# Decoder layer on one core: two stores moved ahead of loads in the SyncE queue, and the VectorE, ScalarE and TensorE lists reordered at the seams and in the last norm

## The reference

```
xn  = rms_norm(x, g_mix);  q, k, v, h, B, C = split(xn @ w_in)
mix = concat(dilated_attention(q, k, v), B * conv3(C * h)) @ w_out
h1  = x + mix
hn  = rms_norm(h1, g_ffn)
y   = h1 + (silu(hn @ w_gate) * (hn @ w_up)) @ w_down
out = rms_norm(y, g_final)
```

## Time and profile before

| | before |
|---|---|
| median of 3 executions | 1271.15 us (1271.0 to 1271.72) |
| the profiled execution, its own time | 1269.17 us |
| span of its instructions | 1267.4 us |
| PE busy | 1228.7 us, 97% of the span |
| DVE, POOL, ACT busy | 46%, 39%, 33% |
| mean granted clock of PE | 0.992 of full speed |
| chain that ended last, by engine | PE 84%, DVE 7%, issue 3%, DMA 2%, ACT 2%, POOL 1% |

### The profile page before, as it was taken

How to read it: one execution, slowest core, us unless ns; L and a number is a source line. 1 busy time by engine, 2 the same in 40 slices (tenths; PEclk the granted TensorE clock), 3 DMA queues, 4 the chain that set the end, 5 groups by cost and what they waited for, 6 DMA issues and landing times.

```text
span 1267.4 us, 22504 instructions
## 1 busy us (share of the span) xinstructions
PE 1228.7 (97%) x9232; PEld 1137.0 (90%) x9232; DVE 579.8 (46%) x982; ACT 418.7 (33%) x806; POOL 494.6 (39%) x414
## 2 busy tenths in 40 slices
PE   7999999999999999999699999999999999999997
PEld 7998778889755599999699999999999999999997
DVE  6844313424666523478233333322111178755665
ACT  6000110000577711255233333333333343444441
POOL 3454023233133132041578777776777650000000
PEclk9999999999999999999799999999999999999999
DMA  5545367353122041001334546454131495222223
GB/s 205 180 167 209 114 221 259 120 185 115 50 67 67 2 172 67 1 26 43 133 123 166 197 159 198 163 183 131 56 101 51 150 353 193 91 92 92 78 75 103
DMA packets 59989, 163.55 MB, mean 129 GB/s; under 512 B 6448, under 2 KB 19952, under 8 KB 55664
## 3 DMA queue, kind: packets, MB, share of 16 engines
q1 hardware_dynamic: 59888, 162.12, 36.9%
HBM read 127.81 MB, written 34.28 MB: 128 GB/s over the span
## 4 chain that ended last, share of the span: by engine, by line
PE 84%; DVE 7%; issue 3%; DMA 2%; ACT 2%; POOL 1%; SPq 1%; DVEq 0%; ACTq 0%; POOLq 0%
PE ps L1283 10%; PE ps L1285 10%; PE ps L1284 10%; PE ps L853 6%; PE ps L855 6%; PE ps L854 6%; PE ps L1309 5%; PE ps L1310 5%; PE ps L1311 5%; PE ps L993 3%; PE ps L1036 3%; PE ps L1060 2%; PE ps L1061 2%; PE ps L1062 2%; PE ps L1015 2%
## 5 line engine op out<-in xcount | busy, mean ns | idle before, releaser
L1283 PE MATMUL ps<-combo,w_hi 128*128 128x264 f32 x672 | 193.0, 287 | 16.2 <-ACT evac L1381 13.8
L1285 PE MATMUL ps<-combo,w_lo 128*128 128x264 f32 x672 | 192.2, 286 | 0.0
L1284 PE MATMUL ps<-combo,w_hi 128*128 128x264 f32 x672 | 192.0, 286 | 0.0
L853 PE MATMUL ps<-act_hi,w_hi 128*128 128x352 f32 x480 | 158.7, 331 | 7.9 <-DVE act_lo L1829 7.9
L855 PE MATMUL ps<-act_hi,w_lo 128*128 128x352 f32 x480 | 154.9, 323 | 0.0
L854 PE MATMUL ps<-act_lo,w_hi 128*128 128x352 f32 x480 | 154.8, 323 | 0.0
L1309 PE MATMUL ps<-hid,w_hi 128*128 128x264 f32 x536 | 152.9, 285 | 1.5 <-DVE resid L2230 1.5
L1310 PE MATMUL ps<-hid,w_hi 128*128 128x264 f32 x536 | 152.4, 284 | 0.0
L1311 PE MATMUL ps<-hid,w_lo 128*128 128x264 f32 x536 | 152.3, 284 | 0.0
L771 POOL TENSOR_TENSOR w_lo<-w_stage,w_hi 128x512 fp32r<-128x512 f32 (+1 forms) x71 | 97.6, 1375 | 138.4 <-ACT w_hi L1381 138.3
L1283 PEld LDWEIGHTS ps<-combo,w_hi 128*128 128x128 f32 x672 | 127.8, 190 | 16.9 <-issue 16.8
(11 more groups left out here) (393 smaller groups left out, 2953.1 us busy)
## 6 DMA issues: line engine op xcount, KB each, us to landing
w_stage<-in_w SPq DMA_DIRECT2D x61, 512.0 KB, 4.2
resid<-in_state_k SPq DMA_DIRECT2D x8, 1792.0 KB, 7.4
v_buf<-in_state_v SPq DMA_DIRECT2D x14, 1024.0 KB, 5.0
h_d<-evac SPq DMA_DIRECT2D x44, 264.0 KB, 3.1
norms<-in_w SPq DMA_DIRECT2D x22, 512.0 KB, 4.3
t_d<-norms SPq DMA_DIRECT2D x11, 1024.0 KB, 7.8
resid<-in_xT SPq DMA_DIRECT2D x16, 528.0 KB, 8.3
raw<-in_w SPq DMA_DIRECT2D x14, 512.0 KB, 4.4
```

The lines of the kernel that those rows point to most:

```text
L853: pe.matmul(out, hi, rhs_hi, start=first, stop=False)
L1283: pe.matmul(out, hi[:, wk], x_hi[:, k, tk], start=(k == 0 and first), stop=False, skip_group_check=not first)
L1284: pe.matmul(out, hi[:, wk], x_lo[:, k, tk], start=False, stop=False, skip_group_check=not first)
L1285: mm = pe.matmul(out, lo[:, wk], x_hi[:, k, tk], start=False, stop=(k == 3), skip_group_check=not first)
```

## The change

The order of work is changed in five places; no operation of the computation is added or removed. (1) At the start of the gate products the SP queue loads gate(2) before it waits for the first SwiGLU values, stores `(1, 0)` and `(1, 1)` ahead of loads that they stood behind, and puts the four `load_sums` transfers behind both stores and two more weight loads. (2) On DVE `plain_hidden` moves from behind six `combined` to behind the first. (3) At the seam to the down product ACT runs `keep_u2` of the last slice before `down_highs(0)` (the rest of the ACT diff there is the same list written out), SP issues `load_hidden("a11", 0)` before two `load_down`, and DVE runs `put_down(0, m)` one step earlier. (4) Under P2, P7 and P4 the squares of quarter 0 move to behind step 49, an ACT square root of one column is added behind step 48, `last_rows(0)` moves from k = 5 to k = 6 and `last_normals(0)` is done in one piece behind step 60. (5) Under the second pass of P4 `last_columns(2)` moves from the end of tile 0 to its step 8, `last_rows(2)` from the end of tile 1 to its step 6, and ACT and DVE take the squares of quarter 2 before the root and mean of quarter 1.

```diff
--- before.py
+++ after.py
@@ -592,16 +592,21 @@
                     source = t_d[k][:, 512 * W_SUMS[product]:512 * W_SUMS[product] + 512]
                 sp.dma_start(down_words(s), source).then_inc(down_in[n % DOWN_RAWS], 16)
 
-            for i in range(4):
+            for i in range(5):
                 load_gate(i)
-            for f in range(1, FT):
+            store_hidden(0, 0)
+            store_hidden(1, 0)
+            load_gate(5)
+            load_gate(6)
+            store_hidden(1, 1)
+            load_gate(7)
+            store_hidden(0, 1)
+            load_gate(8)
+            sp.wait_ge(dve_lo, 32)
+            load_sums(0)
+            load_sums(1)
+            for f in range(3, FT):
                 store_hidden(0, f - 1)
-                if f == 1:
-                    load_gate(4)
-                if f == 2:
-                    sp.wait_ge(dve_lo, 32)
-                    load_sums(0)
-                    load_sums(1)
                 if f < FT - 1:
                     load_gate(2 * f + 3)
                 store_hidden(1, f - 1)
@@ -619,13 +624,13 @@
             split_ready(sp, (FT - 2, "P7"))
             load_down(0)
             load_down(1)
+            sp.wait_ge(gate_done, GATE_NO[FT - 1, "P1"])
+            load_hidden("a11", 0)
             split_ready(sp, (FT - 1, "P5"))
             load_down(2)
             split_ready(sp, (FT - 1, "P6"))
             sp.wait_ge(t_made, 4 * (FT - 1))
             load_down(3)
-            sp.wait_ge(gate_done, GATE_NO[FT - 1, "P1"])
-            load_hidden("a11", 0)
             split_ready(sp, (FT - 1, "P4"))
             load_down(4)
             load_down(5)
@@ -1356,7 +1361,7 @@
                     mm.then_inc(step_done, 1)
                 if k == 3:
                     last_columns(0)
-                if k == 5:
+                if k == 6:
                     last_rows(0)
             down_product(5)
             first_pass(6)
@@ -1365,12 +1370,13 @@
                     mm = down_tile(6 * HK + k, m, 1)
                     if (m, k) == (0, 3):
                         last_columns(1)
+                    if (m, k) == (0, 8):
+                        last_columns(2)
+                    if (m, k) == (1, 6):
+                        last_rows(2)
                 mm.then_inc(tile_done, 1)
                 if m == 0:
                     last_rows(1)
-                    last_columns(2)
-                if m == 1:
-                    last_rows(2)
             final_columns()
             last_rows(3)
 
@@ -1650,35 +1656,33 @@
...
+            keep_p1(FT - 1)
+            weight_high(FT - 1, "P3")
+            silu_first(FT - 1)
+            keep_u2(FT - 1)
+            down_highs(0)
+            down_highs(1)
+            keep_p7(FT - 1)
+            down_highs(2)
+            down_highs(3)
+            silu_second(FT - 1)
+            down_highs(4)
+            down_highs(5)
...
@@ -1713,17 +1717,22 @@
             for n in range(SLOTS, DOWN_STEPS):
                 step = STEP_ORDER[n]
                 down_highs(step)
-                if step in LATE_BEHIND:
-                    late_square(*LATE_BEHIND[step])
-                for q, m in PARTS_BEHIND.get(step, []):
-                    part_square(q, m)
+                for h, m in LATE_BEHIND.get(step, []):
+                    late_square(h, m)
+                if step == 48:
+                    act.activation(r_last[:, 3, 0:1], ones[:, 0:1], ACT.Sqrt)
+                if step == 49:
+                    for m in range(4):
+                        part_square(0, m)
+                for m in PARTS_BEHIND.get(step, []):
+                    part_square(1, m)
                 if step == 57:
                     last_roots(0)
                 if step == 58:
                     last_wide(0)
-            last_roots(1)
             for m in range(4):
                 part_square(2, m)
+            last_roots(1)
             last_wide(1)
             part_square(3, 0)
             last_roots(2)
@@ -2324,12 +2333,12 @@
             combo_low(16, s3_f, S3, 3)
             first_gate(1)
             combined(y21, y21, y22, 0, ALU.add, Y22_AT[0])
+            plain_hidden()
             combined(y21, y21, y22, 1, ALU.add, Y22_AT[1])
             combined(y11, y21, y11, 0, ALU.subtract, S1_AT[0])
             combined(y21, y21, y22, 2, ALU.add, Y22_AT[2])
             combined(y11, y21, y11, 1, ALU.subtract, S1_AT[1])
             combined(y21, y21, y22, 3, ALU.add, Y22_AT[3])
-            plain_hidden()
             combined(y11, y21, y11, 2, ALU.subtract, S1_AT[2])
             combined(y11, y21, y11, 3, ALU.subtract, S1_AT[3])
             for k in range(4):
@@ -2362,50 +2371,52 @@
             for k in range(HK):
                 hidden_sums(k)
                 down_lows(POOL_STEPS + k)
-                if POOL_STEPS + k == HK + 3:
+                if POOL_STEPS + k == HK + 2:
                     for m in range(4):
                         put_down(0, m)
             for n in range(POOL_STEPS + HK, DOWN_STEPS):
                 step = STEP_ORDER[n]
                 i, k = divmod(step, HK)
-                if step == 55:
-                    for m in range(4):
-                        put_part(0, m)
                 down_lows(step)
                 if DOWN_PRODUCTS[i] == "P5":
                     fourth_sum(k)
                 if step in PUTS_BEHIND:
                     for m in range(4):
                         put_down(PUTS_BEHIND[step], m)
-                if step in LATE_BEHIND and LATE_BEHIND[step][1]:
-                    add_late_square(*LATE_BEHIND[step])
-                for q, m in PARTS_BEHIND.get(step, []):
-                    add_part_square(q, m)
+                for h, m in LATE_BEHIND.get(step, []):
+                    if m:
+                        add_late_square(h, m)
+                if step == 49:
+                    for m in range(4):
+                        put_part(0, m)
+                    for m in range(4):
+                        add_part_square(0, m)
+                for m in PARTS_BEHIND.get(step, []):
+                    add_part_square(1, m)
                 if step == 57:
                     last_means(0)
                 if step == 58:
                     last_reciprocals(0)
-                if step == 59:
-                    last_normals(0, range(4))
                 if step == 60:
-                    last_normals(0, range(4, KT))
+                    last_normals(0, range(KT))
                     for m in range(4):
                         put_part(1, m)
             for m in range(4):
                 put_part(2, m)
-            last_means(1)
             for m in range(4):
                 add_part_square(2, m)
+            last_means(1)
             last_reciprocals(1)
             put_part(3, 0)
             last_means(2)
-            last_normals(1, range(4))
+            last_normals(1, range(2))
             last_reciprocals(2)
-            last_normals(1, range(4, KT))
+            last_normals(1, range(2, KT))
             add_part_square(3, 0)
+            last_normals(2, range(4))
             put_part(3, 1)
             add_part_square(3, 1)
-            last_normals(2, range(KT))
+            last_normals(2, range(4, KT))
             put_part(3, 2)
             add_part_square(3, 2)
             put_part(3, 3)
@@ -2532,8 +2543,8 @@
 STEP_ORDER = step_order()
 AT = {x: n for n, x in enumerate(STEP_ORDER)}
 PUTS_BEHIND = {25: 1, 36: 2, 47: 3, 69: 5}
-LATE_BEHIND = {48: (0, 0), 54: (0, 1), 49: (0, 2), 55: (0, 3), 75: (1, 0), 70: (1, 1), 76: (1, 2), 71: (1, 3)}
-PARTS_BEHIND = {56: [(0, m) for m in range(4)], 61: [(1, 0), (1, 1)], 62: [(1, 2), (1, 3)]}
+LATE_BEHIND = {48: [(0, 0)], 54: [(0, 1)], 49: [(0, 2), (0, 3)], 75: [(1, 0)], 70: [(1, 1)], 76: [(1, 2)], 71: [(1, 3)]}
+PARTS_BEHIND = {61: [0, 1], 62: [2, 3]}
 PART_PUT = [TILES[4], TILES[4] + 4, TILES[6], TILES[6] + 4]
 COLUMN_BANK, ROW_BANK = [0, 0, 2], [2, 4, 6, 2]
 
```

More of the change, by code:

```diff
@@ L1652, in _ @@
             keep_u2(2)
-            for f in range(2, FT):
+            for f in range(2, FT - 1):
                 if f > 2:
@@ L1657, in _ @@
                 silu_first(f)
-                if f < FT - 1:
-                    weight_high(f + 1, "P1")
-                else:
-                    down_highs(0)
+                weight_high(f + 1, "P1")
                 if f > 2:
                     keep_u2(f)
-                if f < FT - 1:
-                    weight_high(f + 1, "P2")
-                else:
-                    down_highs(1)
+                weight_high(f + 1, "P2")
                 keep_p7(f)
-                if f < FT - 1:
-                    weight_high(f + 1, "P6")
-                    weight_high(f + 1, "P7")
-                else:
-                    down_highs(2)
-                    down_highs(3)
-                silu_second(f)
-                if f < FT - 1:
-                    weight_high(f + 1, "P5")
-                    weight_high(f + 1, "P4")
-                else:
```

(9 more changed lines are left out.)

## The result

| | before | after |
|---|---|---|
| median | 1271.43 us (4 executions, 1271.0 to 1271.92) | 1246.93 us (4 executions, 1246.81 to 1247.62) |
| the profiled execution, its own time | 1269.17 us | 1246.96 us |
| span | 1267.4 us | 1245.2 us |
| PE busy | 1228.7 us, 97% | 1224.3 us, 98% |
| mean granted clock | 0.992 | 0.998 |

The changed kernel takes 0.9817 of the time of before (95% interval 0.9805 to 0.9829): 24.5 us less. Span against span the gain is 22.2 us. The other 2.3 lie between before's profiled execution and its median.

What follows compares the result with a forecast made beforehand. PE (TensorE) was taken as the bound, so only its late starts could be won: 2.45 + 10.66 - 1.6 + 1.74 + 1.70 + 2.49 + 1.48 = 18.9 us. From 1269.17: 1250.3, plus 1.98: 1252.3 us; range 1247.5 to 1256.5.

Steps and rivals of the forecast that it cites:

- The seam: Idle time before P5(21) and the second down product goes: gains of 1.74 and 1.70 us.
- the margins: Rival: a 0.2 to 0.8 us margin fails, or the clock falls at P4(1) too; 1253.9 to 1255.7 us; chance 0.22.
- the store of (1, 1) was not late: Rival before P5(2): this store still lands late, half of part 2's gain is lost; 1258 to 1263 us; chance 0.05.
- the wait before P5(3) did not recur: Rival: that wait returns in 18 more slices, 2.7 us each, 48 in all; about 1300 us; chance 0.03.
- The landing before P5(3): Store of (1, 2) takes 6.02 us to land, so PE waits 2.7 us in starts, 2.5 idle, before P5(3).
- The clock at P5(3): Charge of 1.6 us for a slower PE clock behind the idle time before P5(3); bounds 0 and 1.6.
- the first rival, the steady clock: The clock does not fall at P5(3): sum 20.5 us, time 1250.7 us; chance 0.22.
- the second, a short landing: Rival: P5(3) does not wait, store of (1, 2) landing under 3.4 us or POOL quicker; 1248.0 us; chance 0.12.
- The base: Median taken as 1.98 us above the profiled execution, added to 1250.3 us to give 1252.3.
- the five later restarts: PE's idle stretches at the seam, second down product, P2 and P4: 1.50, 1.46, 1.54, 0.63, 1.32 us, forecast to go.
- Part 1: Before P4(1): moving `plain_hidden` frees P1(2) of idle time; gain 2.45 us, with a new idle stretch of 1.6.
- The square root ahead: Brings the 1.28 us activation table load to behind step 48, within 3.1 us of cover; charged 0.

Runs made afterwards that it cites:

- a3: Kernel before with only the SP order of the first slices and the place of `plain_hidden` changed; 1254.74 us, 0.9875.
- a1: Changed kernel with the SP queue's old order in the first slices put back; 1261.21 us, 0.9926.
- b3: Changed kernel without the added ACT square root behind step 48; 1246.84 us, 0.9806.
- b4: Changed kernel with the store of (1, 2) issued behind one more load, the gate weights of slice 5; 1251.57 us, 0.9849.
- b1: Changed kernel with the store of (1, 2) put ahead of the load of up weights 4 in the SP queue; 1245.99 us, 0.9799.
- a2: Changed kernel with `plain_hidden` put back behind six `combined`; 1244.96 us, 0.9798.
- d1: Kernel before with only `load_gate(4)` moved ahead of the wait for the first SwiGLU values; 1265.55 us, 0.9969.

## Why the prediction was right, and what it had wrong

The kernel is faster, as forecast, and nearly all of the gain lies where the working put it. The median came 5.4 us below the forecast, 0.6 below its range.

**Right, within 0.2 us.** P4(1) was forecast at 587.80 and starts at 587.81, behind 1.64 us of idle time (1.6). The store of (1, 1) was to go out at 602.2 and goes at 602.28, and P5(2) does not wait. Before P4(2) about 1.0 in starts was forecast, and 0.81 + 0.16 is there. The seam gives 3.47 (3.44), P2 2.66 (2.49), P4 1.5 (1.48), and a3 confirms the three together. The narrowest margin was `last_rows(2)`: its factor is ready at 1223.98 + 0.99 = 1224.97 and PE comes at 1225.24, 0.27 us later (0.3 forecast).

```profile
1223.98 0.99 ACT L1715 ACTIVATE third<-ones,r_last 128x128 f32<-128x128 f32 x3 [0.43 <-DVE r_last L2271]
```

```profile
1225.24 0.49 PE L1188 MATMUL ps<-ident,third 128*128 128x128 f32 x3
```

Of the other rivals none came: the margins held, the store of (1, 1) was not late, and the wait before P5(3) did not recur: POOL caught up, and no restart follows 630.80.

**The landing before P5(3), 1.5 us.** The step was "the landing takes 6.02". The chain ahead of it was right. The working has the store go out at E + 1.4 + 1.24 + 14.48 = E + 17.12; it goes out at 625.56, and 625.56 - 17.12 = 608.44 is the end of P3(1), behind which `first_hidden` starts at 608.48. Then it landed in 4.49 us. The forecast took one row as a fixed price and left its spread out. With the old SP list this transfer landed in 6.02 us (before), 6.03 (a1), 5.68 and 5.29 (the second and third profile of before: 637.11 to 642.79 and 637.15 to 642.44); with the new one in 4.49 (changed kernel), 4.46 (a3) and 4.42 (b3); in b4 in 5.09. With the old list the next load is issued 0.83 us behind the store, with the new one 1.28 or 1.29 us behind, and in b4 two loads stand ahead and none behind. At the same 0.83 us the landing still varies by 0.7 us, so this distance alone does not set it. What does was not separated by a run and stays open. The mechanism of the wait was as forecast: b1 takes it away by issuing this store earlier, and b4 lengthens it by issuing it later.

**The clock at P5(3), 1.6 us.** "The idle time is as long as the 2.42 of the earlier trace rows after which the clock fell" hung on the landing. The idle time was 0.92, and the clock stayed. At 3.23 us, in b4, it fell. So the term of 1.6 us was charged for a wait that came out at a third of its length. This is the first rival, the steady clock, and half of the second, a short landing. Neither alone is what happened: the wait stayed, at a third of its forecast length. With both corrections the sum is 18.9 + 1.5 + 1.6 = 22.0, and the spans differ by 22.2.

**The base, 2.0 us.** The forecast added 1.98 us to the changed kernel's time, because the median of before was so far above its profiled execution. That took the difference for a constant of the kernel. It was the clock behind before's own restarts, which the change removes. The prediction charged no clock for the five later restarts because in its one profile there was none; the two further profiles show it behind three of them in one execution and behind none in another. After the change the executions spread over 0.8 us and the profiled one is at the median. So the 5.4 us between the forecast and the median are 1.5 + 1.6 + 2.0, and the 0.2 of the other rows; 0.1 is left by rounding.

**Part 1 hit the number in part by luck.** Its 2.45 us were credited to the new place of `plain_hidden` alone. The chain that it drew is there: DVE waits at `plain_hidden` until 580.38 (580.45), the last `combined` ends at 585.42 (585.42), and P4(1) starts at 587.81. But in a1, which has the move and not the earlier load, the last `combined` ends at 585.99. The `combined` ahead of `plain_hidden` and the first of the seven behind it run beside POOL there. The latter takes 1.1 us up to the next one, where the forecast took 0.61 from a row in which POOL rests:

```profile
581.11 1.18 DVE L1823 TENSOR_TENSOR norms<-norms,early 128x528 f32<-128x528 f32 x1
```

Counted from the restart at 548 us, P4(1) then starts 0.9 us later than in the changed kernel, the clock falls, and nothing is left of the 2.45 us at P5(2). In the changed kernel the early load of gate(2), which removes the wait of ACT (4.21 us) and DVE (3.35 us) ahead of the list, lets POOL finish before DVE comes to the seven. The price that the forecast had too low did not come to bear because of a load that it did not price. And the move was not needed: a2 and d1 show that with the load alone P1(2) does not wait, and the move costs the changed kernel 2.0 us (a2). The prediction costed the DVE list from rows of before and did not ask what ended DVE's idle time at 573.91. Of the SP edit it looked at the stores, not at the load that was moved with them.

**The square root ahead.** It was charged nothing, and it is worth nothing (b3). The Trainium skill (ScalarE: Activation LUTs, What ACT_TABLE_LOAD costs) adds 1.38 us of drain to the 1.28 of the load. In b3's rows the load takes the 1.28 us and the next ACTIVATE starts 0.01 us after it ends. So this case agrees on the load and shows no drain; the measurement decides.

## What to carry to other kernels

When a queue's list is reordered, follow every transfer that moves, loads too: the gain that was looked for on VectorE's list comes here from one weight load moved ahead of a wait, which alone gives 3.9 us (d1) and gives less together with the move on that list. An instruction moved ahead in an in-order list makes everything behind it wait for what it waits for; first look whether a wait further up the list already explains its lateness. And before adding the gap between a profiled execution and the median to a forecast, profile the kernel again: if the two profiles differ in the granted clock behind the same idle stretches, the gap belongs to those stretches and goes when they go.

## What the runs showed of the hardware

Behind an idle stretch of PE the clock does not fall or stay by its length alone. In before's three profiles it stayed behind 2.56 and 2.54 us and fell behind 2.42, 1.96, 1.54 and 1.33. In a1 it fell behind 2.54, and in a3 it stayed behind 1.89. Behind 1.64 us and less it stayed in the changed kernel; behind 3.23 (b4) and 12.17 us (a1) it fell. Two executions of one kernel differ in this at the same restart, with up to 1.6 us between them. What decides it is open.

A store of the same size from the same line, issued among the same loads, landed in 4.42 to 6.03 us.

A VectorE sum of 128x528 took 1.18 us in a1 beside GpSimd (581.11), and 0.70 us with GpSimd at rest (582.21).
